# Two transformer blocks in fp32 on one core: the rows of the expert layer in eight buffers instead of sixteen, with the power of the query norm behind an earlier gather

## What is computed

```python
# per token: 8 heads, each picks 16 of 16384 experts by two products with 128 keys
q = rms-normed query of the head, split in two halves of 128
s1, s2 = q1 @ keys1.T, q2 @ keys2.T            # 128 scores each
top 16 of each, top 16 of the 16 x 16 sums -> e (16 experts), g = softmax of their scores
a = einsum('cd,ckd->ck', xc, expert_u[ec])      # one dot of 1024 per expert
w = g * gelu(a)
y = einsum('ck,ckd->cd', w, expert_v[ec])       # weighted sum of the v rows
out = h + y
```

## Time and profile before

| | before |
|---|---|
| median of 3 runs | 1464.77 us (1459.92 to 1467.07) |
| span of the profiled execution | 1461.4 us |
| busy PE / DVE / ACT / POOL | 91% / 65% / 38% / 26% |
| DMA, mean over the span | 278 GB/s |
| gathers (`software_dynamic` queue) | 276.60 MB, 46.0% of 16 engines |
| TensorE clock, mean granted | 0.966 |

### The profile page before, as it was taken

The page is one execution under the profiler, slowest core; times in us unless marked ns, Lnnn a source line. Parts: engine busy times, 40 slices in busy tenths (PEclk is TensorE's granted clock), DMA queues, the critical chain, the costliest instruction groups (busy, mean ns, idle before and its releaser), DMA issues.

```text
span 1461.4 us, 19665 instructions
## 1 busy us (share of the span) xinstructions
PE 1326.6 (91%) x6493; PEld 946.6 (65%) x6493; DVE 952.8 (65%) x2289; ACT 551.2 (38%) x1133; POOL 379.2 (26%) x384
## 2 busy tenths in 40 slices
PE   8999999999999999999998889787897989788888
PEld 6988999988988999977787535343343535343333
DVE  4687555564657555585785777776767777776755
ACT  4553544444545444454672222222222212222221
POOL 1104000000000000012642454335444354345440
PEclk9999999999999999999999999899999999999999
DMA  9615655535315555564403999999999999999997
GB/s 364 260 54 125 226 184 183 190 144 231 115 44 173 187 181 192 168 218 132 154 28 118 415 420 421 420 422 421 422 422 421 422 421 421 420 421 422 421 422 310
DMA packets 97535, 406.86 MB, mean 278 GB/s; under 512 B 6955, under 2 KB 44524, under 8 KB 60748
## 3 DMA queue, kind: packets, MB, share of 16 engines
q0 software_dynamic: 39552, 276.60, 46.0%
q1 hardware_dynamic: 57932, 129.60, 25.8%
HBM read 404.84 MB, written 1.07 MB: 278 GB/s over the span
## 4 chain that ended last, share of the span: by engine, by line
PE 50%; DMA 23%; issue 13%; DVE 10%; POOL 2%; ACT 2%; DVEq 0%; POOLq 0%; SPq 0%; ACTq 0%; PEldq 0%
DMA ring<-in_peer_uv,prob 20%; PE ps L688 13%; PE ps L689 12%; PE ps L690 12%; PE ps L841 6%; DMA uv_gain<-in_peer_uv,prob 2%; DMA ring<-in_peer_wq 1%; PE ps L815 1%; PE ps L877 1%; DVE prob L2417 1%; DVE prob L2405 1%; POOL small L1656 1%; PE ps L635 1%; DVE ring L2541 1%; DVE sco L2430 0%
## 5 line engine op out<-in xcount | busy, mean ns | idle before, releaser
L1876 DVE TENSOR_TENSOR w_low<-ring,w_high 128x1024 fp32r<-128x1024 f32 x140 | 165.2, 1222 | 151.3 <-ACT w_high L1220 150.8
L1220 ACT ACTIVATE w_high<-ring 128x1024 fp32r<-128x1024 f32 x142 | 142.7, 1052 | 171.8 <-PE ps L690 171.8
L688 PE MATMUL ps<-hT_high,w_high 128*128 128x256 f32 x512 | 145.0, 283 | 0.9 <-DVE hT_low L1869 0.9
L689 PE MATMUL ps<-hT_low,w_high 128*128 128x256 f32 x512 | 144.9, 283 | 0.0
L690 PE MATMUL ps<-hT_high,w_low 128*128 128x256 f32 x512 | 144.8, 283 | 0.0
L1471 ACT ACTIVATE prob<-prob 128x4 f32<-128x4 f32 (+2 forms) x67 | 13.8, 206 | 346.6 <-DVE prob L2541 346.6
L1459 ACT ACTIVATE sco<-const,prob 128x128 f32<-128x128 f32 x256 | 84.3, 392 | 151.7 <-DVE prob L2551 137.8
L841 PE MATMUL ps<-arena_v,sco 128*128 128x512 f32 x256 | 121.5, 619 | 18.6 <-ACT sco L1459 18.6
L1662 POOL TENSOR_SCALAR small<-small 128x1 f32<-128x1 f32 x8 | 4.3, 533 | 502.0 <-ACT arena_v L1252 502.0
L841 PE MATMUL ps<-ring,sco 128*128 128x512 f32 x192 | 102.4, 684 | 31.4 <-ACT sco L1459 31.4
L841 PE MATMUL ps<-arena_u,sco 128*128 128x512 f32 x256 | 115.7, 601 | 8.3 <-ACT sco L1459 8.3
(11 more groups left out here) (446 smaller groups left out, 3083.8 us busy)
## 6 DMA issues: line engine op xcount, KB each, us to landing
ring<-in_w_up SPq DMA_DIRECT2D x32, 1024.0 KB, 5.5
ring<-in_w_down SPq DMA_DIRECT2D x32, 1024.0 KB, 4.9
qkring<-in_qk_a SPq DMA_DIRECT2D x8, 1024.0 KB, 7.1
qkring<-in_qk_b SPq DMA_DIRECT2D x8, 1024.0 KB, 4.8
ring<-in_peer_wq SPq DMA_DIRECT2D x8, 1024.0 KB, 9.2
ring<-in_w_in SPq DMA_DIRECT2D x8, 860.0 KB, 5.5
ring<-in_w_out_a SPq DMA_DIRECT2D x4, 1024.0 KB, 15.8
ring<-in_v_b SPq DMA_DIRECT2D x4, 1024.0 KB, 7.2
```

Source lines behind the costliest of these rows:

```text
L688: pe.matmul(dst, a[0], b[0], start=start, stop=False, skip_group_check=True)
L689: pe.matmul(dst, a[0], b[1], start=False, stop=False, skip_group_check=True)
L1220: sc.activation(w_split[pair][0][:, part], ring[:, slot, part], ACT.Copy)\
L1876: ve.tensor_tensor(w_split[pair][1][:, part], ring[:, slot, part], w_split[pair][0][:, part].bitcast(F32), ALU.subtract)\
```

## The change

The list of buffers keeps its first eight entries. Step k uses buffer k % 8, and so each buffer twice in a unit. GpSimd's order changes with it. `freed_gather` waits for one count of `v_used` as before, but counts now begin with gather 8 of the first unit: gather k from 8 on waits for step k - 8 of its own unit, and gather k below 8 for step k + 8 of the unit ahead. In the first unit the power stands directly behind `experts_ready`, gathers 8 to 15 each wait for a freed buffer, and the waits for the scaled rows and the keys are gone. In a tile-1 unit the power stands behind gather 3 instead of gather 9. VectorE waits for a landing of 16 per use, two uses per buffer and unit. The other engines' programs keep their order.

```diff
--- before.py
+++ after.py
@@ -63,6 +63,7 @@
 CHOOSE_STEPS = 47
 GROUP = 4
 N_DIAG = 4
+N_SLOTS = 8
 PEER_SLOT = 2
 
 
@@ -313,8 +314,6 @@
                               pieces_r((split_v, 4096), (split_v, 5120))] + v_main]
         slots = [ring[:, 0, :], ring[:, 1, :], ring[:, 3, :], uv_proj[:, :]]
         slots += [au[:, 2048 * r:2048 * r + 2048] for r in range(4)]
-        slots += [av[:, 2048:4096], av[:, 4096:6144], uv_mk[:, 0, :], uv_mk[:, 1, :], uv_gain[:, 0, :], uv_gain[:, 1, :],
-                  av[:, 6144:8192], av[:, 0:2048]]
         keysT = qkring[:, 0, :]
         keysT_first = probT[:, :, :].rearrange("p m n -> p (m n)")[:, 0:2 * P]
         hT_first = relu[:, :, :].rearrange("p a n -> p (a n)").rearrange("p (c s) -> p c s", c=NB)
@@ -839,7 +838,7 @@
                     pe.wait_ge(sem("diag_ready"), count.take("diag_ready"))
                     for n in range(2):
                         last = pe.matmul(ps[2 * t + n][:, :], diag[:, k % N_DIAG, :],
-                                         slots[k][:, D + n * HALF:D + (n + 1) * HALF],
+                                         slots[k % N_SLOTS][:, D + n * HALF:D + (n + 1) * HALF],
                                          start=False, stop=(final and k == TOPK - 1), skip_group_check=True)
                         if final and t == 1 and k == TOPK - 1 and n == 0:
                             last.then_inc(sem("v_used"), 1)
@@ -1789,18 +1788,21 @@
                 po.sem_inc(sem("gathers_due"), 1)
 
             def gather(t, k):
-                po.indirect_dma_start(slots[k], None, T["peer_uv"],
+                po.indirect_dma_start(slots[k % N_SLOTS], None, T["peer_uv"],
                                       bass.IndirectOffsetOnAxis(ap=expert[:, 16 * t + k:16 * t + k + 1], axis=0))\
-                    .then_inc(sem(f"uv{k}_landed"), 16)
+                    .then_inc(sem(f"uv{k % N_SLOTS}_landed"), 16)
+
+            def freed_gather(t, k):
+                po.wait_ge(sem("v_used"), count.take("v_used"))
+                alone()
+                gather(t, k)
 
             def unit(t, power_at=None):
 
                 po.wait_ge(sem("experts_ready"), count.take("experts_ready"))
                 alone()
                 for k in range(TOPK):
-                    po.wait_ge(sem("v_used"), count.take("v_used"))
-                    alone()
-                    gather(t, k)
+                    freed_gather(t, k)
                     if k == power_at:
                         power(ms_out[:, 0:2], ms_in[:, 0:2], "ms_ready", "rms_ready")
 
@@ -1816,19 +1818,15 @@
                     gather(0, k)
                 po.wait_ge(sem("experts_ready"), count.take("experts_ready"))
                 alone()
-                for k in range(8, 12):
-                    gather(0, k)
                 power(ms_out[:, 1:2], ms_in[:, 1:2], "ms_ready", "rms_ready")
-                po.wait_ge(sem("rows_scaled"), count.take("rows_scaled"))
-                po.wait_ge(sem("keysT_ready"), count.take("keysT_ready", 6))
-                for k in range(12, TOPK):
-                    gather(0, k)
+                for k in range(N_SLOTS, TOPK):
+                    freed_gather(0, k)
 
             first_unit()
-            unit(1, power_at=9)
+            unit(1, power_at=3)
             with count.loop(P_HEADS - 2, experts_ready=2, v_used=32, ms_ready=1):
                 unit(0)
-                unit(1, power_at=9)
+                unit(1, power_at=3)
             unit(0)
             unit(1)
 
@@ -2536,8 +2534,9 @@
 
             def dot(t, k):
 
-                ve.wait_ge(sem(f"uv{k}_landed"), count.take(f"uv{k}_landed", 16))
-                row = slots[k][:, 0:D]
+                n = k % N_SLOTS
+                ve.wait_ge(sem(f"uv{n}_landed"), count.take(f"uv{n}_landed", 16))
+                row = slots[n][:, 0:D]
                 ve.tensor_tensor_reduce(row, row, nat[:, t, :], 1.0, 0.0, ALU.mult, ALU.add, dots[:, k:k + 1])\
                     .then_inc(sem("dot_done"), 1)
 
@@ -2627,7 +2626,7 @@
                 first_query_rms(1)
                 unit(0, more=True, first=True)
                 unit(1)
-                per = {f"uv{k}_landed": 32 for k in range(TOPK)}
+                per = {f"uv{n}_landed": 2 * 16 * (TOPK // N_SLOTS) for n in range(N_SLOTS)}
                 with count.loop(P_HEADS - 2, gate_w_ready=2, gelu_ready=8, rms_ready=1, key_scores_done=1,
                             peer_sq_done=1, v_chain=CHOOSE_STEPS, **per):
                     unit(0, more=True)
```

## The result

The change takes 1616.38 us (median) beside 1464.68 us for the kernel before on the same chip, a ratio of 1.1045 (95% interval 1.1019 to 1.1072). That is 152 us slower; 1529 us were forecast, 64.5 us slower, and 1616 lies above the range of 1488 to 1570. One of the four executions (1774 us, mean TensorE clock 0.77 instead of 0.93) fell in a slower state and is left out. The profiled execution took 1615.61 us; its span is 1613.7 us.

A forecast was written before the change was run, and what follows sets the result against it. A DMA queue that must never run dry was taken as the bound. 7.8 us a pair over 7.5 pairs gave 58.5, plus 8 for the opening, minus 2 at the end: 64.5 us slower, 1529 us, range 1488 to 1570.

The forecast's parts named there:

- a plain group fits, with 1.0 us to spare: Group of four at full clock: first bytes 6.4 us after the closing landing, against 7.5 us of work in flight.
- holes at every group with TensorE at full clock: Sign against the forecast: the queue running dry at every group would mean the 4.7 or 1.7 us were mis-sized.
- The restart: DMA queue after running dry: slow first 2 us cost between 0 and 1.1 us, taken as 0.5 each time.
- Tile 1, group 0 to 3: Choice of next experts delays dot 4, first expert at half clock: dry 2.6 us, 3.1 a pair with restart.
- Tile 0, the key queries: Key queries of half 1 between experts 1 and 2 delay a gather: dry 1.8 us, 2.3 a pair with restart.
- The other six groups: Rest of a pair: none late at full clock, each 1.2 us at half clock; two counted, 2.4 us a pair.
- the third rival: TensorE at half clock in most groups: 17.4 us a pair, 1600 us, or 1575 with half of it; chance 10%.
- The power at 0: GpSimd's power behind gather 3 of tile 1: fits by 1.8 us, taken as nothing, at half clock up to 1.5.
- The opening at 8 us: First unit, gather 8 waits for the first expert: dry 9.1 us, up to 2.7 back, 8 taken.
- The end at -2: Last unit has no choice between its dots and weighs smaller groups: 2 us gained.
- The first: Rival: three gathers in flight cover everything but the opening, 1465 to 1473 us; chance 6%.
- The second: Rival: only the two choice groups lose, at full clock without restart loss, 2.7 us a pair, 1490 to 1505; chance 22%.

The follow-up runs named there:

- Half of each product left out: The change, with TensorE leaving out the second 512 of 1024 output columns in all units but the last two: 1591.40 us, ratio 1.0872.
- four products of zeros: The change, with TensorE adding four products with zeros behind each group of four to keep its clock up: 1603.38 us, ratio 1.0953.
- distances 8, 9, 10 and 12: Kernel before with sixteen buffers, each gather waiting for the step 8, 9, 10 or 12 earlier: 1614.40, 1523.06, 1472.81 and 1464.42 us.
- the power alone: Kernel before with sixteen buffers, only GpSimd's two powers moved as in the change: 1464.73 us beside 1464.50, ratio 0.9995.
- distance 10: Kernel before with sixteen buffers, each gather waiting for the step ten earlier, five in flight when a group closes: 1472.81 us, ratio 1.0058.
- the filled kernels: The change, with two or four products with zeros added on TensorE behind each group of four: 1609.89 us and 1603.38 us.

## Why the prediction was wrong

**What held.** The bound (a queue that must not run dry), the loop that eight buffers close, three in flight at the closing landing, GpSimd waiting nearly always for L840 (359.9 of its 393.8 us of idle time from 900 to 1500), and a landing after 8 to 12 us (median 8.7). The sign was right.

**The step that failed: "a plain group fits, with 1.0 us to spare."** The forecast compared 4.7 + 1.7 = 6.4 us to the first bytes with 3 x 2.49 = 7.5 us of work. In the terms of the table this claims that a gather into an empty queue lands 1.7 + 2.49 = 4.2 us after its issue. No gather of the trace did that: the shortest landing in the earlier trace rows was 5.8 us, and with it the same sum is 4.7 + 5.8 = 10.5 us against 9.96. After, the shortest in the chain is 5.41, which makes 10.1. The row was at hand and was used only against the estimate of 4.4 us. The runs put 6.87 in the place of 4.2 and 5.75 in that of 4.7. So no group is plain: each of the eight in a pair takes 12.6 us instead of the 10.3 that 82.1/8 makes, 2.35 more, 19 a pair, where 7.8 were forecast. Half of each product left out shows that it is the landing: with the way to the issue at the forecast's 4.7, the period is 12.15 all the same. The prediction had named this sign itself, holes at every group with TensorE at full clock, for a 4.7 or a 1.7 that was mis-sized. The kernel with four products of zeros shows just that, and the 4.7 stood. So did the 1.7, nearly: in the turn above the first packet starts 1.85 us after the issue at 1080.34. What failed is that first bytes in time do not make the landing come in time.

**Why the landing is longer.** Cover was counted to the end of the last engine. A landing is the slowest engine's; the quickest ran dry 4.6 us behind it in the hole above, and idles while the queue as a whole still moves. The packet records further show slow packets: from 900 to 1400 us, 9.0% of those of 8 KB took over 0.4 us (up to 2.0) where the usual is 0.31, and this is the 10% of slower transfers. With four in flight it was 4.5%, with five 0.7%, with seven and in the kernel before 0.02%. Of the 19 us a pair, about 11 are idle share (0.11 x 101) and 8 busy time that was not there before (0.90 x 101 - 1.01 x 82.1). The slow packets go with a gather that an engine comes to early. Counting 128 packets to a gather in order of start, an estimate since the engines are not in step, 88% of those that start less than 2 us after their gather's issue took over 0.4 us, and 7% of those that start 3.5 to 4 us after it. This points to the supply of a gather's packets more than to the engines' being out of step, but no run separates the two, and the cause stays open. What the runs do show is that the number in flight decides, over five kernels (the change and distances 8, 9, 10 and 12) that differ in little else.

**The restart, taken as 0.5 us (0 to 1.1) for each dry spell,** was the size in which this belonged. Set against 2.35 us more in every group, it was too small by nearly 2 us and had too few places: the 16 groups with a way to the issue below 5 us took 12.99 us on average, the 39 with a longer one 12.47.

**Tile 1, group 0 to 3, 3.1 us a pair:** the mechanism is there (1074.09, half clock, a hole from 1079 to 1082), and it is one of eight alike. **Tile 0, the key queries, 2.3 us a pair,** 16 for seven pairs: 10.7 measured by moving them. **The other six groups, 2.4 us a pair, for two at half clock:** 39 of 55 groups had a way to the issue above 5 us, so half speed became as common as the third rival said. But the price was wrong: with the clock at 1.00 the kernel gains 13 us. A late issue meets an emptier queue and lands faster (6.31 us in those 39 groups, 8.25 in the 16).

**The power at 0:** held, by a run of its own and by VectorE's waits. **The opening at 8 us:** 11 measured, with the dry spell from 817.7 to 825.1 us as forecast (817 to 826); the 2.7 us that might have come back did not, and the power alone gave nothing either. **The end at -2** was not tried by itself. No gain shows in the trace: the last unit took 43.1 us from its first dot to its last instead of 38.5.

**The rivals.** The first (everything covered but the opening, 1465 to 1473) is what distance 10 does, at 1472.81; it needs five in flight, not three. The second (two groups a pair) is refuted by the period of the others. The third came nearest in time, 1575 to 1600, and is refuted as the cause by the filled kernels. Its lower value does not follow from its own terms: half of 17.4 us a pair gives about 1536 us, and all of it with half the restarts 1568. Faster was excluded. The page of the Trainium skill on "DMA: Bandwidth & Descriptors", section "Anatomy of one DMA", from whose rule 4.4 us of a landing were estimated, is contradicted again: the shortest piece in the chain from 900 to 1500 us is 5.41 us, the mean of the table 6.87. The forecast's own 4.2 us was no better than that estimate.

**What a reader could have seen.** The earlier trace rows give a test in one line: full pace needs (in flight + 1) x 2.49 us to exceed the way to the issue plus the shortest landing. With three it is 9.96 against 10.5. That alone is 0.5 us a group and 4.3 a pair: the direction in every group, but not the size. Nor does passing the test suffice. Four in flight pass it with 12.45 against 5.56 + 5.8 = 11.4 and lost 58 us, because the landings grew to 8.40; only the kernels with more in flight showed how many are enough.

## What to carry to other kernels

When buffers limit a stream of transfers, count how many are in flight at the moment that frees the next ones, not how many buffers there are: eight buffers released in groups of four, one dot late, were three in flight. Then close the loop with a *landing* from the trace (issue to consumer), not with bytes over rate, and count cover to the first engine of the queue that empties. That test can only warn: a kernel that fails it will lose, one that passes it may lose too. Here transfers of 1 MB were 58 us short of full pace with four in flight and came near it with five, 12.5 us of work against a way to the issue of 5.5 us; shortening that way with half products or raising TensorE's clock gave back 25 and 13 us of 152.

## What the runs showed of the hardware

- The rate of these gathers depended on how many were in flight when the next were freed: 339, 386, 418 and 421 GB/s for 3, 4, 5 and 7. The step from 3 to 4, a whole transfer of cover (2.49 us), did not bring full pace.
- At a shallow queue the engines' busy time for the same bytes grew too: 377 GB/s per full share with 3 in flight, 386/0.97 = 398 with 4, 418/1.01 = 414 with 5, 417 with 7.
- A gather's completions on the sixteen engines lay 3.1 us apart in the steady queue of before (around 960 to 1075 us). In the change it was 0.4 to 0.8 us for most gathers right behind a dry spell (0.69 at 1086), and up to 3.0 us later in a batch (the landing at 1074).
- Packets of 8 KB took 0.31 us, and over 0.4 us in 9.0, 4.5, 0.7 and 0.02% of cases with 3, 4, 5 and 7 gathers in flight.
- TensorE's clock can be held at 1.00 by products with zeros in its pauses (464 instead of 381 us busy of 500); in a kernel whose queue is the bound it gave back 13 of 1616 us.
